# The last mixer of a two-block network: the blocks of one weight matrix in another order, with the attention levels and the convolution's taps placed between them

## The chip, the cores and the metric

The kernel runs on one core of one Trainium2 chip. The core has five engines that run side by side, each through a list of instructions of its own: TensorE (PE in the profile), VectorE (DVE), ScalarE (ACT), GpSimd (POOL) and SyncE (SP, which here only issues DMAs). They meet at semaphores. The metric is the device time of one execution in microseconds. The kernel before took 2451.9 us, the median of three runs between 2444.78 and 2456.0.

## The reference

Two blocks run after each other over 256 tokens of width 1024. The first (two layers of feed-forward, state-space scan and dilated attention) and the experts at the end of the second are not touched here. The change lies in the mixer of the second block:

```python
def hybrid_mixer(u, w_in, w_dw, ...):      # u: 256 tokens x 1024, normalised
    # one product u @ w_in gives: the convolution's input (1024 columns), q and k (512 each),
    # v (1024), r (1024), a low-rank gate (16), the gates of both branches (2048)

def conv_module(u, w_dw, b_dw, ln_g, ln_b, w_pw, b_pw):
    a, gt = jnp.split(u, 2, axis=-1)
    z = a * jax.nn.sigmoid(gt)
    # 31 taps along the tokens, each of the 512 channels by itself, + b_dw
    z = jax.nn.silu(layernorm(z, ln_g, ln_b))
    return z @ w_pw + b_pw

def gla_chunked(q, k, v, logg):            # linear attention, 4 heads, dk 128, dv 256
    b = jnp.cumsum(gc, axis=2)
    diff = b[:, :, :, None, :] - b[:, :, None, :, :]
    decay = jnp.exp(jnp.where(causal, diff, -jnp.inf))
    attn = jnp.einsum("bhid,bhijd,bhjd->bhij", qc, decay, kc)
    o = jnp.einsum("bhij,bhje->bhie", attn, vc)   # and the state that is carried on
```

The output of the attention is divided by its root mean square in each head, multiplied by a gain and by silu(r), and sent through w_gla_o. Both branches are multiplied by their sigmoid gates, added, and sent through w_out.

## The kernel before

Everything in this stage is float32; most activations lie with channels on the 128 partitions and the 256 tokens along each partition. Weights come as blocks of 1024x256 (1 MB) through a ring of four slots (`ring`); SP issues the load of block n+4 once PE has released the slot of block n. PE writes its products to four PSUM banks (`misc`) in a fixed order of "fills", which the list `fills` at the start of `two_blocks` sets: fill m goes to bank m modulo 4, and PE claims it (`claim_bank`) only when fill m-4 has been read out, by ACT or by DVE. No scheduler takes part: each engine's order is the order in which its code is written.

The mixer's parts, by the names in the code:

- **a1, a2** are the low-rank decay. From it DVE and ACT make the log of the decay (`decays2`; ACT's Exp and Ln, then a running sum of 8 scans at L2207, `bcum`).
- **w_in2** is the product with w_in, 24 blocks of 16 matmuls (the profile counts each float32 matmul as two): four of q and k (`qk2`), four of v (`v2`), four of the convolution's input and its gate (`pc`), four of r, eight of gates. ACT reads each out (`evac`).
- **The levels.** The decay between two tokens of a chunk is not one product of a factor per row and one per column that stays in range, so it is built in seven levels (`LEVELS`, halves of 64, 32, ... 1 tokens), one level for the diagonal, and one for what crosses the two halves of 128 tokens (`cross`). For a level DVE takes differences of `bcum` (L2221, L2222), ACT makes their exponential (L1613, `decay_exp`), DVE multiplies them into keys and queries (L2238, L2239), PE forms the products of all pairs (L1040, `pairs`: two fills of four heads), and DVE copies those that the level's mask lets through into `attn` (L2266). `lev_e` and `lev_qk` have two buffers, so level s+2 waits for the products of level s.
- **The taps** (`gated`, L2249 and L2254): 31 taps for each of four groups of channels, 124 instructions on DVE, each waiting for the last one of its own group.
- **o, osum**: the attention's output (L1057 to L1060, read out by ACT at L1651), its squares (DVE, L2278) and their sums by a matmul with ones (L1068). DVE then makes the reciprocal (L2288) and applies it and the gain (L2293, L2296).
- **mean, var**: two matmuls with ones (L1077) for the layer norm of the convolution, with DVE (L2305 to L2317) and ACT (L1658, L1661) around them. Then come the convolution's second product (`pw`, L1089), that of the attention (`ygla`, L799), the merge on DVE, and w_out (L1115).

In the code before, PE goes through all 24 blocks of w_in2, and then through `gla` and the start of `conv_branch`. DVE makes two levels, waits for the pc blocks, does all its 124 taps, and then does the levels that are left one after the other, each with PE and ACT in turn.

Of the kernel before, what the change touches and what calls it, by code (L numbers as in the profile page):

```python
# [8 lines left out]
U32 = mybir.dt.uint32  # L9
ALU = mybir.AluOpType  # L10
# [3 lines left out]
P = 128  # L14
# [35 lines left out]
GH = 4  # L50
# [78 lines left out]
def two_blocks(nc, d, out):  # L129
    fills = []  # L130
    slots, rows_d = [], []
    for l in range(DEPTH):
# [6 lines left out]
        for j in range(8):  # L139
# [8 lines left out]
    fills += [(("mod", 4 * DEPTH - 1), 1), (("norm", U1), 4), ("a1", 1), ("a2", 2), ("qk2", 4), ("v2", 4), ("pc", 4), ("r", 4), ("gates", 8),  # L148
              ("pairs", 2 * len(LEVELS) + 2), ("cross", 1), ("o", GH), ("osum", 2),
              ("mean", 1), ("var", 1), (("pwa", 0), 1), (("pwb", 0), 1), (("pwa", 1), 1), (("pwb", 1), 1), ("ygla", 4), ("garow", 2), (("norm", U1 + 1), 4), ("router", 1),  # L150
# [8 lines left out]
    with ctx:  # L159
# [412 lines left out]
        def _(sp):  # L572
# [111 lines left out]
        def _(pe):  # L684
# [315 lines left out]
            def w_in2():  # L1000
# [5 lines left out]
                for j in range(4):  # L1006
                    cols_out(FILL["qk2"] + j, n0 + j, 0, 0)
# [9 lines left out]
                for j in range(4):  # L1017
                    toks_out(FILL["v2"] + j, n0 + 4 + j, 0, 0)
                for j in range(4):
                    cols_out(FILL["pc"] + j, n0 + 8 + j, 0, 0)  # L1020
                for j in range(4):
                    cols_out(FILL["r"] + j, n0 + 12 + j, 0, 0)
                with pe.Fori(0, 2) as i:
                    for j in range(4):
                        cols_out(FILL["gates"], n0 + 16, i, j)

            def gla():
                for s in range(len(LEVELS) + 1):
                    if s < len(LEVELS):
                        pe.wait_ge(lev_qk_ready, s + 1)  # L1030
                    for t in range(NT):
                        b = claim_bank(FILL["pairs"] + 2 * s + t)
                        for h in range(GH):
                            if s < len(LEVELS):
                                keys = lev_qk[:, s % 2, h * SEQ + t * P:h * SEQ + (t + 1) * P]
                                queries = keys
                            else:
                                keys = q2k2[:, GH + h, t * P:(t + 1) * P]
                                queries = q2k2[:, h, t * P:(t + 1) * P]
                            mm = pe.matmul(b[:, h * P:(h + 1) * P], keys, queries, start=True, stop=True)  # L1040
                        mm.then_inc(filled, 1)
# [7 lines left out]
                for i in range(2 * len(LEVELS) + 2):  # L1049
                    if i >= 2 * len(LEVELS) - 2:  # L1050
                        wait_drained(pe, FILL["pairs"] + i)
                wait_drained(pe, FILL["cross"])
                for h in range(GH):
# [8 lines left out]
                    mm.then_inc(filled, 1)  # L1062
                pe.wait_ge(o_sq, 1)
# [7 lines left out]

            def conv_branch():
                for k, (name, src) in enumerate((("mean", zc), ("var", zsq))):
                    pe.wait_ge(z_out, k + 1)
                    b = claim_bank(FILL[name])
                    for c in range(NC2):
                        mm = pe.matmul(b[:, 0:SEQ], ones[:, :], src[:, c, :], start=(c == 0), stop=(c == NC2 - 1))  # L1077
                    mm.then_inc(filled, 1)
# [236 lines left out]
            gla()  # L1315
# [78 lines left out]
        def _(act):  # L1394
# [220 lines left out]
            def w_in2():  # L1615
                m, n0 = FILL["a1"], RING["win2"]
                wait_filled(act, m)
                act.activation(a1T[0:RANK, :], bank_of(m)[0:RANK, 0:SEQ], ACT.Copy).then_inc(drained[m % 4], 1)
                for j in range(4):
                    evac(FILL["qk2"] + j, n0 + j, q2k2[:, 2 * j:2 * j + 2, :], 2,  # L1620
                         scale=DK ** -0.5 if j < 2 else 1.0)
                for j in range(4):
                    evac(FILL["v2"] + j, n0 + 4 + j, v2[:, :, j * BLK:(j + 1) * BLK], 2)
                    if j == 0:

                        act.wait_ge(gl_ready, 1)
                        s = step(act.activation(lev_e[:, 0, :], lev_e[:, 0, :], ACT.Exp))
                        act.wait_ge(act_step, s)
                        act.activation(lev_e[:, 0, :], lev_e[:, 0, :], ACT.Ln, bias=1.0).then_inc(gl_log, 1)
                for s in range(2):  # L1630
                    decay_exp(s)
                for j in range(4):
                    evac(FILL["pc"] + j, n0 + 8 + j, pc[:, 2 * j:2 * j + 2, :], 2,
                         ACT.Copy if j < 2 else ACT.Sigmoid)
                for j in range(4):
                    evac(FILL["r"] + j, n0 + 12 + j, rT[:, 2 * j:2 * j + 2, :], 2, ACT.Silu)
                with act.Fori(0, 2) as i:
                    for j in range(4):
                        m = FILL["gates"] + j
                        wait_slot_read(act, n0 + 16, i, j)  # L1640
                        act.activation(gT[:, bass.ds(i * 8 + 2 * j, 2), :],
                                       bank_of(m).rearrange("p (a b) -> p a b", a=2), ACT.Sigmoid)\
                            .then_inc(drained[m % 4], 1)

            def gla():
                for s in range(2, len(LEVELS) + 1):
                    decay_exp(s)
# [8 lines left out]
            def conv_branch():  # L1656
                act.wait_ge(var2, 2)
                act.activation(mean, mean, ACT.Sqrt).then_inc(std2, 1)  # L1658
                act.wait_ge(zn_ready, 1)
                for c in range(NC2):  # L1660
                    ins = act.activation(zc[:, c, :], zc[:, c, :], ACT.Silu, scale=colb[:, B_LG + c:B_LG + c + 1],  # L1661
                                         bias=colb[:, B_LB + c:B_LB + c + 1])
                ins.then_inc(zs_ready, 1)
# [120 lines left out]
            gla()  # L1784
            conv_branch()
# [21 lines left out]
        def _(dve):  # L1807
# [375 lines left out]
            def decays2():  # L2183
# [26 lines left out]
                for j in range(4):  # L2210
                    wait_drained(dve, FILL["qk2"] + j)

            def level(s):
# [3 lines left out]
                if s < len(LEVELS):  # L2217
# [3 lines left out]
                    dve.tensor_tensor(ev[:, :, 0:w], mid, bv[:, :, 0:w], ALU.subtract)  # L2221
# [486 lines left out]
```

## Time and profile before

| | |
|---|---|
| median of three runs | 2451.9 us (2444.78 to 2456.0) |
| the profiled execution, whole | 2441.12 us |
| its span, first to last instruction | 2439.3 us |
| PE busy over the span | 2252.6 us, 92% |
| VectorE busy | 1617.8 us, 66% |
| ScalarE busy | 1033.5 us, 42% |
| TensorE's granted clock, mean | 0.961 of full speed |

The profiled execution took 1.8 us more than its span and lies 3.7 us under the fastest of the three runs. In the views below, times are microseconds from the start of the span. A busy share says how long an engine had work in flight, and not that this work set the end. What sets it is read from idle time in front of an instruction, and from what released it (in square brackets in a timeline).

### The profile page before, as it was taken

What the parts mean: (1) busy time and instruction counts of PE and PEld (TensorE: products, weight loads), DVE (VectorE), ACT (ScalarE), POOL (GpSimd) and SP (SyncE); (2) the same over time, 40 slices, a digit from 0 to 9 for tenths busy, and PEclk for the clock granted to TensorE, in tenths of its full rate; (3) what the DMA queues carried; (4) which work ended last, traced back from release to release, by engine and by line L of the source; (5) the groups of instructions that cost most, each with busy time, mean ns of one, the idle gap of its engine ahead of it and who ended that gap; (6) DMA issues with size and microseconds to landing.
All of it is one profiled execution on the core that took longest, in us unless ns stands there. A gap on an engine that the chain in (4) does not pass through costs nothing.

```text
span 2439.3 us, 36349 instructions
## 1 busy us (share of the span) xinstructions
PE 2252.6 (92%) x14222; PEld 1966.0 (81%) x14222; DVE 1617.8 (66%) x2299; ACT 1033.5 (42%) x1209; POOL 440.2 (18%) x227
## 2 busy tenths in 40 slices
PE   5999899999999999999999899859589999999996
PEld 5998897579989988985799788746278888888885
DVE  5655877376576648783766417351488888888887
ACT  3332343244343423432433221110167777777773
POOL 8403471052044034620430000000000000000000
PEclk8999999999999999999999999969699999999998
DMA  8765563166657555541665354304169999999993
GB/s 245 234 194 159 166 196 121 52 228 220 203 179 236 179 166 175 185 144 52 207 215 178 115 155 149 110 0 138 69 200 318 323 315 333 313 331 318 321 326 120
DMA packets 354783, 481.06 MB, mean 197 GB/s; under 512 B 12528, under 2 KB 311808, under 8 KB 354704
## 3 DMA queue, kind: packets, MB, share of 16 engines
q1 hardware_dynamic: 341568, 443.58, 55.8%
q0 software_dynamic: 10496, 34.25, 4.3%
q10 hardware_dynamic: 2640, 2.14, 0.3%
q8 instruction: 54, 0.88, 0.2%
q14 instruction: 25, 0.20, 0.0%
HBM read 478.88 MB, written 1.05 MB: 197 GB/s over the span
## 4 chain that ended last, share of the span: by engine, by line
PE 80%; DVE 14%; ACT 4%; issue 1%; DMA 1%; DVEq 0%; ACTq 0%
PE misc L687 11%; PE misc L689 11%; PE misc L688 11%; PE misc L799 8%; PE acc L957 4%; PE misc L1167 4%; PE misc L1168 4%; PE acc L687 3%; PE acc L689 3%; PE acc L688 3%; PE misc L1153 3%; PE acc L1205 3%; DVE arena L1990 2%; PE misc L1180 2%; DVE ring_low L1874 2%; DVE ring_low L2476 1%
## 5 line engine op out<-in xcount | busy, mean ns | idle before, releaser
L687 PE MATMUL misc<-xl,high_b 128*128 128x256 f32 x1408 | 395.1, 281 | 15.7 <-DVE ring_low L1874 15.7
L688 PE MATMUL misc<-xh,ring_low 128*128 128x256 f32 x1408 | 393.6, 280 | 0.0
L689 PE MATMUL misc<-xh,high_b 128*128 128x256 f32 x1408 | 393.5, 279 | 0.0
L2476 DVE TENSOR_TENSOR ring_low<-ring,high_b 128x2048 fp32r<-128x2048 f32 x128 | 287.4, 2288 | 53.8 <-ACT high_b L1670 53.8
L687 PEld LDWEIGHTS misc<-xl,high_b 128*128 128x128 f32 x1408 | 266.7, 189 | 20.0 <-issue 14.0
L688 PEld LDWEIGHTS misc<-xh,ring_low 128*128 128x128 f32 x1408 | 267.2, 190 | 3.3
L689 PEld LDWEIGHTS misc<-xh,high_b 128*128 128x128 f32 x1408 | 267.9, 190 | 0.0
L1167 PE MATMUL misc<-high_b,ue 128*128 128x256 f32 x1024 | 250.7, 286 | 18.3 <-DVE ring_low L2476 18.3
L799 PE MATMUL misc<-xnT,ring 128*128 128x256 f32 x1152 | 251.9, 381 | 0.0
L1168 PE MATMUL misc<-ring_low,ue 128*128 128x256 f32 x1024 | 247.6, 283 | 0.0
L799 PEld LDWEIGHTS misc<-xnT,ring 128*128 128x128 f32 x1152 | 220.0, 191 | 30.3 <-issue 0.8
L1670 ACT ACTIVATE high_b<-ring 128x2048 fp32r<-128x2048 f32 x128 | 237.8, 1910 | 0.4
L1874 DVE TENSOR_TENSOR ring_low<-ring,high_b 128x2048 fp32r<-128x2048 f32 x88 | 221.4, 2557 | 24.0 <-ACT high_b L1438 24.0
L1469 ACT ACTIVATE arena<-arena 128x256 f32<-128x256 f32 x88 | 36.8, 418 | 435.3 <-DVE arena L1908 435.3
L1167 PEld LDWEIGHTS misc<-high_b,ue 128*128 128x128 f32 x1024 | 195.6, 191 | 24.9 <-issue 21.2
L1168 PEld LDWEIGHTS misc<-ring_low,ue 128*128 128x128 f32 x1024 | 196.2, 192 | 1.6 <-issue 0.2
L1384 POOL TENSOR_SCALAR arena<-arena,cact 128x1024 f32<-128x1024 f32 x56 | 193.5, 3456 | 4.7 <-DMA arena<-in_w_ada_f_dram 1.2
L1381 POOL TENSOR_SCALAR arena<-arena,cact 128x1024 f32<-128x1024 f32 x8 | 26.1, 3261 | 774.6 <-PE misc L997 768.1
L1438 ACT ACTIVATE high_b<-ring 128x2048 fp32r<-128x2048 f32 x88 | 163.1, 1902 | 0.0
L1908 DVE TENSOR_TENSOR arena<-misc,row_rstd 128x256 f32<-128x256 f32 x88 | 37.2, 422 | 188.0 <-PE misc L689 182.2
L1386 POOL TENSOR_TENSOR arena<-arena 128x1024 f32<-128x1024 f32 x56 | 160.1, 2858 | 4.7
L687 PE MATMUL misc<-ring_low,xh 128*128 128x256 f32 x512 | 148.1, 289 | 0.0
(362 smaller groups left out, 4660.9 us busy)
## 6 DMA issues: line engine op xcount, KB each, us to landing
ring<-in_w_dram SPq DMA_DIRECT2D x128, 1024.0 KB, 8.6
ring<-in_w_in_dram SPq DMA_DIRECT2D x72, 1024.0 KB, 5.6
ring_d<-in_w_dram SPq DMA_DIRECT2D x128, 512.0 KB, 4.9
ring<-in_ffn_w_gate_dram SPq DMA_DIRECT2D x44, 1024.0 KB, 5.5
ring<-in_ffn_w_up_dram SPq DMA_DIRECT2D x44, 1024.0 KB, 7.9
ring_d<-in_ffn_w_down_dram SPq DMA_DIRECT2D x88, 512.0 KB, 7.5
arena<-in_w_ada_dram POOLq DMA_DIRECT2D x48, 512.0 KB, 4.9
ring<-in_w_out_dram SPq DMA_DIRECT2D x20, 1024.0 KB, 4.9
```

The costliest lines, as they stand in the source:

```text
L687: pe.matmul(dst, wh, ml, start=start, stop=False, **kw)
L688: pe.matmul(dst, wl, mh, start=False, stop=False, **kw)
L689: return pe.matmul(dst, wh, mh, start=False, stop=stop, **kw)
L799: mm = pe.matmul(b[:, c * SEQ:(c + 1) * SEQ], w[:, k, c * P:(c + 1) * P], src[:, k, :], start=(k == 0), stop=(k == KD - 1))
L1167: pe.matmul(dst, ue[:, k, half, :], high_part(n)[:, k, :], start=(k == 0), stop=False)
L1168: mm = pe.matmul(dst, ue[:, k, half, :], low_part(n)[:, k, :], start=False, stop=(k == KD - 1))
L1384: pool.tensor_scalar(row, row, cact[:, k:k + 1], None, ALU.mult).then_inc(pool_step, 1)
L1386: pool.tensor_tensor(ada, ada, row, ALU.add).then_inc(ada_used, 1)
L1438: act.activation(high_b[:, s, :], ring[:, s, :], ACT.Copy).then_inc(high_in[s], 1)
L1670: act.activation(high_b[:, s, :], ring[:, s, :], ACT.Copy).then_inc(high_in[s], 1)
L1874: dve.tensor_tensor(ring_low[:, s, :], ring[:, s, :], high_b[:, s, :].bitcast(F32), ALU.subtract)\
L2476: dve.tensor_tensor(ring_low[:, s, :], ring[:, s, :], high_b[:, s, :].bitcast(F32), ALU.subtract)\
```

## The change

The same instructions are issued in another order, on PE, ACT and DVE alike; in SP's list of loads the four blocks pc and the four blocks v2 trade places. On PE the blocks pc come before the blocks v2. After each of these eight blocks stands one level's pair of fills, `cross` stands between the blocks r0 and r1, the attention's output after r1, the sums of squares after r3, and the two matmuls of the layer norm behind the third and the fifth block of the gates. DVE makes a level in two parts (`level(s, 0)`, the differences, and `level(s, 1)`, the products) with the copies of the level before the last between them, and takes the taps in portions: 10 at each of levels 4 to 7, then 12, 32 and the last 40. ACT's exponentials stand between its read-outs. The loops over the eight blocks of gates are written out. The diff, cut to its core:

```diff
-    fills += [(("mod", 4 * DEPTH - 1), 1), (("norm", U1), 4), ("a1", 1), ("a2", 2), ("qk2", 4), ("v2", 4), ("pc", 4), ("r", 4), ("gates", 8),
-              ("pairs", 2 * len(LEVELS) + 2), ("cross", 1), ("o", GH), ("osum", 2),
+    fills += [(("mod", 4 * DEPTH - 1), 1), (("norm", U1), 4), ("a1", 1), (("qk2", 0), 1), ("a2", 2)]
+    fills += [(("qk2", j), 1) for j in range(1, 4)]
+    for k in range(len(LEVELS) + 1):
+        fills += [(("pc" if k < 4 else "v2", k % 4), 1), (("pairs", k), 2)]
+    fills += [(("r", 0), 1), ("cross", 1), (("r", 1), 1), ("o", GH), (("r", 2), 1), (("r", 3), 1), ("osum", 2)]
+    fills += [(("gates", j), 1) for j in range(3)] + [("mean", 1), (("gates", 3), 1), (("gates", 4), 1), ("var", 1)]
+    fills += [(("gates", j), 1) for j in range(5, 8)]
...
-                load_block(n0 + 4 + j, 0, 0, w_in, V0 + j * BLK)
+                load_block(n0 + 4 + j, 0, 0, w_in, j * BLK)
             for j in range(4):
-                load_block(n0 + 8 + j, 0, 0, w_in, j * BLK)
+                load_block(n0 + 8 + j, 0, 0, w_in, V0 + j * BLK)
...
+                for k in range(len(LEVELS) + 1):
+                    if k < 4:
+                        cols_out(FILL["pc", k], n0 + 4 + k, 0, 0)
+                    else:
+                        toks_out(FILL["v2", k - 4], n0 + 4 + k, 0, 0)
+                    pairs(k)
+                cols_out(FILL["r", 0], n0 + 12, 0, 0)
+                cross()
+                cols_out(FILL["r", 1], n0 + 13, 0, 0)
+                attended()
+                cols_out(FILL["r", 2], n0 + 14, 0, 0)
+                cols_out(FILL["r", 3], n0 + 15, 0, 0)
+                squares()
+                for j in range(8):
+                    cols_out(FILL["gates", j], n0 + 16 + j, 0, 0)
+                    if j == 2:
+                        moment(0, "mean", zc)
+                    if j == 4:
+                        moment(1, "var", zsq)
...
+            def attended():
+                for k in range(len(LEVELS) + 1):
+                    for t in range(NT):
+                        wait_drained(pe, FILL["pairs", k] + t)
+                for j in range(4):
+                    wait_drained(pe, FILL["v2", j])
...
+                qk2_out(0)
+                qk2_out(1)
+                act.wait_ge(gl_ready, 1)
+                s = step(act.activation(lev_e[:, 0, :], lev_e[:, 0, :], ACT.Exp))
+                act.wait_ge(act_step, s)
+                act.activation(lev_e[:, 0, :], lev_e[:, 0, :], ACT.Ln, bias=1.0).then_inc(gl_log, 1)
+                qk2_out(2)
+                decay_exp(0)
+                decay_exp(1)
+                qk2_out(3)
                 for j in range(4):
+                    evac(FILL["pc", j], n0 + 4 + j, pc[:, 2 * j:2 * j + 2, :], 2, ACT.Copy if j < 2 else ACT.Sigmoid)
+                    decay_exp(j + 2)
                 for j in range(4):
+                    v2_out(j)
+                    if j < 2:
+                        decay_exp(j + 6)
+                r_out(0)
+                r_out(1)
                 for h in range(GH):
                     m = FILL["o"] + h
                     wait_filled(act, m)
                     act.activation(oT[:, 2 * h:2 * h + 2, :], bank_of(m).rearrange("p (a b) -> p a b", a=2),
                                    ACT.Copy).then_inc(drained[m % 4], 1)
+                r_out(2)
+                r_out(3)
                 act.wait_ge(var2, 1)
                 act.activation(rgs, rg, ACT.Sqrt).then_inc(std2, 1)
...
+            def level(s, part_):
...
+            def branches():
+                level(0, 0)
+                level(1, 0)
                 for j in range(4):
+                    wait_drained(dve, FILL["qk2", j])
+                level(0, 1)
+                level(1, 1)
                 last = [0] * NC2
+                taps = iter([(k, c) for k in range(CONV_W) for c in range(NC2)])
+
+                def convolve(n):
...
+                for k in range(len(LEVELS) + 1):
+                    if k + 2 <= len(LEVELS):
+                        dve.wait_ge(lev_qk_ready, k + 1)
+                        level(k + 2, 0)
+                    if k == 4:
+                        for j in range(4):
+                            wait_drained(dve, FILL["pc", j])
+                        link(dve.tensor_tensor(zpad[:, :, CONV_W - 1:], pc[:, 0:NC2, :], pc[:, NC2:2 * NC2, :],
+                                               ALU.mult))
+                    if k >= 4:
+                        convolve(10)
                     for t in range(NT):
+                        m = FILL["pairs", k] + t
                         wait_filled(dve, m)
                         dve.copy_predicated(attn[:, t * GH:(t + 1) * GH, :],
+                                            masks[:, k:k + 1, :].bitcast(U32).to_broadcast([P, GH, P]),
                                             bank_of(m).rearrange("p (a b) -> p a b", a=GH))\
                             .then_inc(drained[m % 4], 1)
                         wait_drained(dve, m)
+                    if k + 2 <= len(LEVELS):
+                        level(k + 2, 1)
+                convolve(12)
                 m = FILL["cross"]
                 wait_filled(dve, m)
                 dve.tensor_copy(across.rearrange("p a b -> p (a b)"), bank_of(m)).then_inc(drained[m % 4], 1)
+                convolve(32)
                 for h in range(GH):
                     wait_drained(dve, FILL["o"] + h)
                 dve.tensor_tensor(osq, oT, oT, ALU.mult).then_inc(o_sq, 1)
+                convolve(CONV_W * NC2)
+                after_step(last[NC2 - 1])
+                dve.nop().then_inc(z_out, 1)
```

On PE, from the first product of w_in2 to the second product of the convolution, the list before reads as follows. L1004 and L1014 are a1 and a2, L799 and L810 blocks of w_in2 (16 matmuls each), L1040 the levels' pairs, L1046 `cross`.

```order
L1004 MATMUL misc<-xnT,wa 16x256 x8
L799 MATMUL misc<-xnT,ring 128x256 x16
L1014 MATMUL misc<-arena,wa 128x256 x4
L799 MATMUL misc<-xnT,ring 128x256 x48
L810 MATMUL misc<-ring,xnT 128x256 x64
L799 MATMUL misc<-xnT,ring 128x256 x128
L1023 UNCONDITIONAL_BRANCH
L1023 ISA
L695 REGISTER_ALU
L799 MATMUL misc<-xnT,ring 128x256 x48
...
L1040 MATMUL misc<-arena 128x128 x64
L1046 MATMUL misc<-arena 128x128 x4
```

In the changed kernel (six lines further down in the file: L805 and L816 are the blocks, L1058 the pairs, L1066 `cross`, L1094 the sums of squares, L1102 mean and var) the same place reads, from the four blocks of q and k on:

```order
L805 MATMUL misc<-xnT,ring 128x256 x64
L1058 MATMUL misc<-arena 128x128 x8
L805 MATMUL misc<-xnT,ring 128x256 x16
L1058 MATMUL misc<-arena 128x128 x8
...
L805 MATMUL misc<-xnT,ring 128x256 x32
L1094 MATMUL misc<-arena,ones 128x256 x8
L805 MATMUL misc<-xnT,ring 128x256 x48
L1102 MATMUL misc<-arena,ones 128x256 x4
L805 MATMUL misc<-xnT,ring 128x256 x32
L1102 MATMUL misc<-arena,ones 128x256 x4
L805 MATMUL misc<-xnT,ring 128x256 x48
L1116 MATMUL misc<-arena,ring 128x256 x32
```

The 64 pairs that stood in one piece behind all blocks now stand in eights between them, and three blocks of gates stand between the last small product and pw (L1116).

On DVE, the place where the taps stood, before (L2246 is the gated input, L2249 and L2254 the taps, L2266 the masked copies):

```order
L2239 TENSOR_TENSOR arena<-arena 128x16x32
L2246 TENSOR_TENSOR arena<-arena 128x4x256 [waits drained3,drained0,drained2,drained1]
L2249 TENSOR_SCALAR arena<-arena,colc,colb 128x256 [waits dve_step]
L2249 TENSOR_SCALAR arena<-arena,colc,colb 128x256 x3
L2254 SCALAR_TENSOR_TENSOR arena<-arena,colc 128x256 [waits dve_step] x120
L2266 COPY_PREDICATED arena<-arena,misc 128x512 [waits dve_step,filled,masks_in]
L2266 COPY_PREDICATED arena<-arena,misc 128x512 [waits filled,drained1]
L2221 TENSOR_TENSOR arena<-arena 128x32x16 [waits drained2]
```

And changed, around level 4 (L2305 is the gated input, L2288 and L2292 the taps, L2312 the masked copies, L2270 and L2271 a level's second part, L2258 and L2260 the first part of `cross`):

```order
L2305 TENSOR_TENSOR arena<-arena 128x4x256 [waits drained3,drained2,drained0,drained1]
L2288 TENSOR_SCALAR arena<-arena,colc,colb 128x256 [waits dve_step]
L2288 TENSOR_SCALAR arena<-arena,colc,colb 128x256 x3
L2292 SCALAR_TENSOR_TENSOR arena<-arena,colc 128x256 [waits dve_step] x6
L2312 COPY_PREDICATED arena<-arena,misc 128x512 [waits filled]
L2312 COPY_PREDICATED arena<-arena,misc 128x512 [waits filled,drained2]
L2270 TENSOR_TENSOR arena<-arena 128x512 [waits filled,lev_exp,drained3]
L2271 TENSOR_TENSOR arena<-arena 128x512
L2258 TENSOR_TENSOR arena<-arena 128x4x128 [waits lev_qk_ready]
L2260 COPY arena<-arena 128x4x128
L2292 SCALAR_TENSOR_TENSOR arena<-arena,colc 128x256 [waits dve_step] x10
```

The first ten taps now stand between two levels, ahead of the copies of level 4; four levels have been through before the first of them.

## Rows read from the trace of the kernel before

**Rows 1.** The page: busy time (share) of each engine, and the granted clock in 40 slices.

```profile
PE 2252.6 (92%) x14222; PEld 1966.0 (81%) x14222; DVE 1617.8 (66%) x2299; ACT 1033.5 (42%) x1209; POOL 440.2 (18%) x227
...
PEclk8999999999999999999999999969699999999998
```

**Rows 2.** Stretches of the span: length, each engine's busy time (instructions), granted clock, DMA.

```profile
core 0: us, PE busy (x) PEld busy (x) DVE busy (x) ACT busy (x) POOL busy (x), PEclk, DMA share, GB/s
1400.00:1562.00 162.00, 162.00 (x750) 142.32 (x749) 61.94 (x147) 26.94 (x34) 0.00 (x0) 1.00 0.48 149
1562.00:1639.00 77.00, 39.32 (x218) 35.03 (x217) 49.14 (x61) 16.49 (x20) 0.00 (x0) 0.73 0.04 14
...
1580.00:1597.00 17.00, 11.81 (x67) 11.13 (x65) 13.36 (x21) 3.17 (x3) 0.00 (x0) 0.70 0.00 0
...
1639.00:1656.00 17.00, 16.73 (x64) 14.29 (x65) 2.63 (x6) 0.22 (x1) 0.00 (x0) 0.82 0.20 62
1656.00:1684.00 28.00, 27.84 (x129) 24.20 (x128) 5.15 (x9) 0.00 (x0) 0.00 (x0) 1.00 0.46 150
```

**Rows 3.** Timeline of PE: start, length, line, tiles, count, idle before and releaser.

```profile
1401.37 1.99 PE L1014 MATMUL misc<-arena,wa 16*128 16x256 f32 x8
1403.29 20.99 PE L799 MATMUL misc<-xnT,ring 128*128 128x256 f32 x96
1424.11 27.79 PE L810 MATMUL misc<-ring,xnT 128*128 128x256 f32 x128
...
1562.24 3.73 PE L1040 MATMUL misc<-arena 128*128 128x128 f32 x32
1568.83 2.74 PE L1040 MATMUL misc<-arena 128*128 128x128 f32 x16 [2.85 <-DVE arena L2239]
...
1606.87 5.41 PE L1068 MATMUL misc<-arena,ones 128*128 128x256 f32 x16 [3.11 <-DVE arena L2278]
...
1629.32 3.78 PE L1077 MATMUL misc<-arena,ones 128*128 128x256 f32 x8 [15.31 <-DVE arena L2308]
1639.28 16.94 PE L1089 MATMUL misc<-arena,ring 128*128 128x256 f32 x64 [6.17 <-ACT arena L1661]
1656.05 27.79 PE L799 MATMUL misc<-arena,ring 128*128 128x256 f32 x128
```

**Rows 4.** Timeline of DVE, same columns.

```profile
1437.84 2.64 DVE L2207 TENSOR_TENSOR_SCAN arena<-arena 128x128 f32<-128x128 f32 x8
...
1483.23 47.59 DVE L2254 SCALAR_TENSOR_TENSOR arena<-arena,colc 128x256 f32<-128x256 f32 x120
1563.40 0.74 DVE L2266 COPY_PREDICATED arena<-arena,misc 128x512 f32<-128x512 uint32 x1 [32.59 <-PE misc L1040]
...
1567.49 0.69 DVE L2238 TENSOR_TENSOR arena<-arena 128x512 f32<-128x512 f32 x1 [1.12 <-ACT arena L1613]
1568.10 0.68 DVE L2239 TENSOR_TENSOR arena<-arena 128x512 f32<-128x512 f32 x1
...
1614.17 6.55 DVE L2288 RECIPROCAL arena<-arena 128x1024 f32<-128x1024 f32 x1 [1.17 <-ACT arena L1654]
1620.76 2.36 DVE L2293 TENSOR_TENSOR arena<-arena 128x1024 f32<-128x1024 f32 x2
1623.16 3.26 DVE L2296 SCALAR_TENSOR_TENSOR arena<-arena,colb 128x256 f32<-128x256 f32 x8
```

**Rows 5.** Timeline of ACT, same columns.

```profile
1417.40 0.60 ACT L1608 ACTIVATE arena<-misc 128x512 f32<-128x512 f32 x1 [6.31 <-PE misc L799]
...
1431.83 1.28 ACT L1627 ACT_TABLE_LOAD   x1
1433.13 1.06 ACT L1627 ACTIVATE arena<-arena 128x1024 f32<-128x1024 f32 x1
...
1637.15 2.07 ACT L1661 ACTIVATE arena<-arena,colb 128x256 f32<-128x256 f32 x4 [1.78 <-DVE arena L2317]
```

**Rows 6.** DMA issues between 1380 and 1700: count, KB each, median time to landing.

```profile
ring<-in_w_in_dram SPq DMA_DIRECT2D x20, 1024.0 KB, 5.4
```

More of the change, by code:

```diff
@@ new lines, in w_in2, with pairs @@
+                squares()
[5 more added lines that the diff above has]
+                        moment(1, "var", zsq)
+            def pairs(k):
+                if k == len(LEVELS):
+                    for j in range(4):
+                        wait_drained(pe, FILL["qk2", j])
+                else:
+                    pe.wait_ge(lev_qk_ready, k + 1)
+                for t in range(NT):
+                    b = claim_bank(FILL["pairs", k] + t)
+                    for h in range(GH):
+                        if k < len(LEVELS):
+                            keys = lev_qk[:, k % 2, h * SEQ + t * P:h * SEQ + (t + 1) * P]
+                            queries = keys
+                        else:
+                            keys = q2k2[:, GH + h, t * P:(t + 1) * P]
+                            queries = q2k2[:, h, t * P:(t + 1) * P]
+                        mm = pe.matmul(b[:, h * P:(h + 1) * P], keys, queries, start=True, stop=True)
+                    mm.then_inc(filled, 1)
@@ L1042, in gla, with cross @@
+            def cross():
                 pe.wait_ge(lev_qk_ready, len(LEVELS) + 1)
@@ L1070, in gla, with moment @@
                     mm.then_inc(filled, 1)
-            def conv_branch():
[L1073 to L1078, printed above, removed]
+            def moment(k, name, src):
+                pe.wait_ge(z_out, k + 1)
+                b = claim_bank(FILL[name])
+                for c in range(NC2):
+                    mm = pe.matmul(b[:, 0:SEQ], ones[:, :], src[:, c, :], start=(c == 0), stop=(c == NC2 - 1))
+                mm.then_inc(filled, 1)
+            def conv_branch():
                 pe.wait_ge(zs_ready, 1)
@@ L1618, in w_in2, with qk2_out, v2_out, r_out @@
                 act.activation(a1T[0:RANK, :], bank_of(m)[0:RANK, 0:SEQ], ACT.Copy).then_inc(drained[m % 4], 1)
+                def qk2_out(j):
+                    evac(FILL["qk2", j], n0 + j, q2k2[:, 2 * j:2 * j + 2, :], 2, scale=DK ** -0.5 if j < 2 else 1.0)
+                def v2_out(j):
+                    evac(FILL["v2", j], n0 + 8 + j, v2[:, :, j * BLK:(j + 1) * BLK], 2)
+                def r_out(j):
+                    evac(FILL["r", j], n0 + 12 + j, rT[:, 2 * j:2 * j + 2, :], 2, ACT.Silu)
@@ L1632, in w_in2 @@
[L1632 to L1643, printed above, removed]
@@ L1652, in gla @@
                                    ACT.Copy).then_inc(drained[m % 4], 1)
+                r_out(2)
+                r_out(3)
                 act.wait_ge(var2, 1)
                 act.activation(rgs, rg, ACT.Sqrt).then_inc(std2, 1)
[L1656 to L1663, printed above, removed]
+                for j in range(8):
+                    evac(FILL["gates", j], n0 + 16 + j, gT[:, 2 * j:2 * j + 2, :], 2, ACT.Sigmoid)
+                    if j == 4:
+                        act.wait_ge(var2, 2)
+                        act.activation(mean, mean, ACT.Sqrt).then_inc(std2, 1)
+                    if j == 6:
+                        act.wait_ge(zn_ready, 1)
+                        for c in range(NC2):
+                            ins = act.activation(zc[:, c, :], zc[:, c, :], ACT.Silu,
+                                                 scale=colb[:, B_LG + c:B_LG + c + 1],
+                                                 bias=colb[:, B_LB + c:B_LB + c + 1])
+                        ins.then_inc(zs_ready, 1)
             def gathered_experts():
@@ L2260, in gla @@
-            def gla():
-                dve.wait_ge(masks_in, 16)
-                for s in range(len(LEVELS) + 1):
+                taps = iter([(k, c) for k in range(CONV_W) for c in range(NC2)])
+                def convolve(n):
+                    for k, c in itertools.islice(taps, n):
+                        if k == 0:
+                            last[c] = step(dve.tensor_scalar(zc[:, c, :], zpad[:, c, 0:SEQ], colc[:, c:c + 1],
+                                                             colb[:, B_DW + c:B_DW + c + 1], ALU.mult, ALU.add))
+                        else:
+                            after_step(last[c])
+                            last[c] = step(dve.scalar_tensor_tensor(
+                                out=zc[:, c, :], in0=zpad[:, c, k:k + SEQ],
+                                scalar=colc[:, k * NC2 + c:k * NC2 + c + 1], in1=zc[:, c, :],
+                                op0=ALU.mult, op1=ALU.add))
@@ L2657, in _ @@
             decays2()
-            level(0)
-            level(1)
-            gated()
-            gla()
-            conv_branch()
+            branches()
             merge()
```

98 lines of the change are left out of this document (21 added, 77 removed).

## The prediction

> **What bounds the kernel now.** I read four views, each narrower than the last. First the page: TensorE (PE) is busy 92% of the span, and of the 40 slices of 61 us only the first, the last and two behind the middle (0.6 each, the 27th and the 29th) have a granted clock under 0.9 [rows 1]. The reader is to see where PE is not at speed: the 27th slice begins at 1586 us and lies in the stage of this change, the 29th behind w_out. Second the stretches: from 1400 to 1562 us PE works without a gap at clock 1.00, while VectorE (DVE) is busy 61.94 of 162 us and ScalarE (ACT) 26.94; from 1562 to 1639 PE is busy 39.32 of 77 us, at a mean clock of 0.73, and DVE 49.14 [rows 2]. So first PE alone sets the pace beside a DVE that idles, and then a chain of DVE, ACT and PE does, in turns. Third PE's own timeline: twenty blocks of w_in2 run from 1424.11 to 1562.24, 138.13 us or 6.907 each (32 counted matmuls, 0.216 each); then come the levels with an idle of 2.85 us before one of them, and later idles of 3.11, 15.31 and 6.17, each released by DVE or ACT, before pw starts at 1639.28 [rows 3]. Fourth DVE's and ACT's timelines. The 120 multiply-add taps take 47.59 us in one piece, 0.397 each; then DVE waits 32.59 us for the first pairs, which it could have had long before, since PE came to them only behind all 24 blocks [rows 4]. The two long engines' works are laid end to end, not beside each other.
>
> **What PE has to do, in either order.** The change removes and adds no matmul. Behind the twenty blocks stand, by counted instructions: eight levels of 16 and cross with 8 (136), the output with 48, the sums of squares with 16, mean and var with 8 each. At full clock the 128-column kind takes 3.73/32 = 0.117 us [rows 3], so 184 x 0.117 = 21.5; the 256-column kind 0.216, so 32 x 0.216 = 6.9. Together 28.4 us. Today PE needs 1639.28 - 1562.24 = 77.0 for them. If PE never waits in the new order, pw starts at 1562.24 + 28.4 = 1590.6, which is 48.7 earlier. Then pw itself: 64 matmuls take 16.77 us today (1639.28 to 1656.05), because they start at a lowered clock (0.82, [rows 2]); at 0.216 they take 13.8. That is another 3.0. Sum 51.6 us.
>
> **Does PE wait in the new order?** I follow the new lists with durations from the rows. The times are on the axis of before, which holds up to 1410.
>
> The start. ACT reads out the second block of q and k at 1410.5 (one block ahead of the read-out at 1417.40, [rows 5]) until 1411.1. Exp and Ln stand right behind it now, not behind the first v block. From the Exp's start to the scans' start it is 1437.84 - 1433.13 = 4.7 us [rows 4, 5]; with the table load of 1.28 ahead, the scans start at 1417.1 and end 2.64 later, at 1419.8. Four differences at the spacing of 0.61 (1567.49 to 1568.10) end at 1422.2, the two exponentials at about 1423.4, the fourth read-out at 1424.9, and the products of level 0 at 1426.2. PE comes to the first pairs at 1424.1 + 6.9 = 1431.0: 4.8 us to spare.
>
> The levels. PE takes 6.91 + 16 x 0.117 = 8.8 us for a block and a level. DVE has in it two differences (1.2), two copies (1.5, [rows 4]), two products (1.2): 3.9 us; from level 4 on also 10 taps (4.0), and once the gated input (about 1.2): 9.1 at the worst, 7.9 at the next. Level k+2 is ready some 3 to 4 us after the pairs of level k, and PE wants it two blocks and one level later, 15.7 us: about 12 to spare. PSUM is the other hold: a block claims the bank of the fill four before, which is the second copy of the level before the last, done 7 us earlier. What I price at nothing here (10 + 10 + 10 + 10 taps, 16 us, inside a queue for which PE waits) is hidden by the 8.8 us that PE itself takes per level; without that cover the taps would fall on PE one for one.
>
> The tail. PE: eight levels end at 1494.3, r0 1501.2, cross 1502.2, r1 1509.1, output 1514.7, r2 and r3 1528.5, squares' sums 1532.0, three gates 1552.7, mean 1554.4, two gates 1568.2, var 1569.9, three gates 1590.6. DVE: 12 taps and the copy of cross to 1502.9, 32 taps to 1515.6, squares to 1517.9 (wanted at 1528.5), 40 taps to 1533.8 (mean wants them at 1552.7), then the reciprocal 6.55, products 2.36 and gain 3.26 [rows 4] to about 1548.7, wanted by ygla after 1604. Mean's work on DVE, some 3 us, ends near 1557.3 and var wants it at 1568.2. Behind var stands today an idle of 6.17, of which 2.07 are the Silu [rows 3, 5]: so the normalised input is there at about 1574. The Silu, though, stands behind the read-out of the seventh gate block (1584.5): with table load 1.28 and 2.07 it ends at 1587.9, and pw wants it at 1590.6. **2.7 us to spare, the thinnest place of all.** The queue behind that waiting ACT instruction holds only the last gates' read-out, for which DVE's merge waits after pw's first fills.
>
> **Weights.** pc and v2 are loaded in the new order by SP, equal in size. 1 MB lands in 5.4 us [rows 6]; a slot released is needed again three blocks, 20.7 us, later. Eight blocks now have 8.8 us each instead of 6.9, which asks less of the queue; pw, ygla and w_out follow without the pause they had, at one MB in 6.9 us as w_in2 always had at DMA share 0.48 [rows 2]. No term.
>
> **What the trace doesn't show** is PE going back and forth between blocks and small matmuls. The nearest row is a2: 8 instructions of the 256-column kind between two blocks take 1403.29 - 1401.37 = 1.92, where 8 x 0.216 = 1.73 [rows 3]. So 0.19 us per inserted piece, 13 pieces, 2.5 us at one end; at the other the 0.117 contains the last matmul's drain, and overlapped pieces would give back up to 1.5. I take nothing, since between pieces without a wait the rows show none.
>
> The Trainium skill (ScalarE: Activation LUTs, What ACT_TABLE_LOAD costs) says a switch of function set costs a load of about 1.28 us and a drain of about 1.38 on top. Here the Exp starts 1.30 us after its load starts [rows 5]: load yes, drain no. By the page the Silu would end 1.4 us later, still ahead of PE, so the sum is the same and the thin place thinner.
>
> **Sum.** 2441.12 - 51.6 = 2389.5 us for an execution like the profiled one. That one lay 10.8 under the median of the runs; on the median's scale it is 2451.9 - 51.6 = 2400.3. I say 2400.
>
> **Rivals.**
> - *The convolution's tail is late* (0.08). The Silu's place has 2.7 us; a DVE that falls more than 10 us behind, or an ACT that falls 3 behind, makes PE wait there. For it: the DVE queue is one file, and a tap waits for its own predecessor. Against: every link up to the Silu has over 10 us. Price: the last idle of 6.17 comes back and with it pw's lowered clock (3.0): 2409.4. All of the last two idles (15.31 as well) would give 2424.8; 0.02 for that.
> - *Slower: PE's clock falls in the mixed stretch* (0.03). Where PE stops briefly for each level, its mean clock is 0.70, between its two levels of 1.2 and 2.4 GHz (1580 to 1597, [rows 2]). If PE stopped at the levels for a moment each time, the big blocks would run at the low clock too. The work from 1424.11 to the end of pw is 138.1 + 28.4 + 13.8 = 180.3 us at full clock and takes 231.9 today; it breaks even at a mean clock of 0.78. At 0.70 it takes 257.6: 25.7 later, 2477.6. Against: it needs stops, and I find none above; while fed, the clock stays at 1.00 for 162 us. The Trainium skill (TensorE: Matmul & The Clock Gate, A second HAM failure mode) tells of just this, brief idles between groups that cycle through PSUM banks making the clock swing. The small idles with a clock of 0.70 agree; the blocks, which also cycle through the four banks, do not.
> - *No change* (0.02): weights come late as PE no longer pauses, and the gain goes into waits for slots. It would take 51.6/30 = 1.7 us at each of the 30 blocks from pc to w_out, so landings of over 22 us instead of 5.4. 2452.
>
> **Numbers.** The forecast has 0.85. About 0.5%, 12 us, is what a measurement of this kernel tells from no change. The forecast's own spread: the runs lie from 7 under to 4 over their median, the switches cost up to 2.5. Low end 2389, where runs come out like the profiled one; high end 2414, which takes in the late tail with the runs' 4 us. Faster 0.95 (forecast and tail), same 0.02, slower 0.03.
>
> **What would show it.** Right: PE at clock 1.00 without an idle over 1 us from 1401 to the end of ygla, the twenty blocks and the small pieces in about 167 us, pw in 13.8, DVE's taps in five or more portions with the first before the copies of level 4, and the stages behind w_out as long as before. Wrong: an idle of PE before a level's pairs (start too late), before pw (the Silu), a granted clock under 1.00 beside blocks, or a longer expert stage.

## The result: 2386.4 us against 2448.3, just under the range

The changed kernel took 2386.41 us (median of four runs, 2381.95 to 2391.17); the kernel before, now with four runs, 2448.34 (2439.75 to 2456.0). The ratio is 0.9748, with an interval of 0.9708 to 0.9789. That is faster, as forecast, but 13.6 us under the predicted 2400 and 2.6 us under the low end of the range. The profiled execution of the changed kernel took 2391.17 us, where the sum for an execution like the profiled one had been 2389.5. That they lie so close is in part luck: this execution came to the stretch that the change touches 4.3 us later than the profiled one of before (1405.67 against 1401.37).

The page of the changed kernel, busy time and granted clock. They answer to [rows 1]:

```profile
PE 2244.2 (94%) x14222; PEld 1962.4 (82%) x14222; DVE 1615.0 (68%) x2299; ACT 1038.7 (43%) x1213; POOL 443.5 (19%) x227
...
PEclk8999999999989999999999989999699999999998
```

The instruction counts of PE and DVE are the same as before; ACT has four table loads more. One of the two slices at clock 0.6, the 27th, is gone; the two new eights (12th and 24th slice) come from ahead of the changed stretch, which begins at 1405.67, inside the 24th, and has clock 1.00 throughout. The stretch from a2 to the start of the attention's second product (L805 on oT, "ygla"), in both kernels; columns as in [rows 2]. Before:

```profile
1401.37:1656.05 254.68, 216.73 (x1025) 190.73 (x1025) 113.71 (x214) 43.66 (x54) 0.00 (x0) 0.91 0.33 103
```

After:

```profile
1405.67:1607.81 202.14, 202.14 (x1025) 180.14 (x1025) 113.60 (x214) 48.34 (x58) 0.00 (x0) 1.00 0.42 130
```

The same 1025 matmul records, and the same 113.6 us of DVE; but PE is busy for all of the 202.14 us, at clock 1.00. The stretch is 52.54 us shorter: 37.95 us are idle that PE no longer has (254.68 - 216.73), and 14.59 are busy time (216.73 - 202.14), the same matmuls at clock 1.00 instead of a mean of 0.91. Where [rows 3] showed idles of 2.85, 3.11, 15.31 and 6.17, PE's timeline after the change shows none (excerpts; L805 and L816 are the blocks, L1058 the levels, L1102 mean and var, L1116 pw):

```profile
1407.59 27.89 PE L805 MATMUL misc<-xnT,ring 128*128 128x256 f32 x128
1435.32 1.95 PE L1058 MATMUL misc<-arena 128*128 128x128 f32 x16
1437.11 7.07 PE L805 MATMUL misc<-xnT,ring 128*128 128x256 f32 x32
1444.01 1.95 PE L1058 MATMUL misc<-arena 128*128 128x128 f32 x16
...
1571.55 1.89 PE L1102 MATMUL misc<-arena,ones 128*128 128x256 f32 x8
1573.28 20.88 PE L805 MATMUL misc<-xnT,ring 128*128 128x256 f32 x96
1594.00 13.98 PE L1116 MATMUL misc<-arena,ring 128*128 128x256 f32 x64
1607.81 27.79 PE L805 MATMUL misc<-arena,ring 128*128 128x256 f32 x128
```

No row has a bracket, which would show an idle of PE. A level costs PE 1.79 us (1435.32 to 1437.11), and pw 13.81 where it took 16.77. DVE around level 4, where the taps begin (L2305 gated input, L2288 and L2292 taps, L2312 masked copies), answers to [rows 4]:

```profile
1467.07 1.22 DVE L2305 TENSOR_TENSOR arena<-arena 128x1024 f32<-128x1024 f32 x1
1468.33 1.38 DVE L2288 TENSOR_SCALAR arena<-arena,colc,colb 128x256 f32<-128x256 f32 x4
1469.62 2.46 DVE L2292 SCALAR_TENSOR_TENSOR arena<-arena,colc 128x256 f32<-128x256 f32 x6
1472.00 1.48 DVE L2312 COPY_PREDICATED arena<-arena,misc 128x512 f32<-128x512 uint32 x2
...
1482.82 4.04 DVE L2292 SCALAR_TENSOR_TENSOR arena<-arena,colc 128x256 f32<-128x256 f32 x10
1488.57 0.73 DVE L2312 COPY_PREDICATED arena<-arena,misc 128x512 f32<-128x512 uint32 x1 [1.71 <-PE misc L1058]
```

The idle in the brackets has changed sides: DVE now waits for PE, by 1.71 us in the last row. Only at level 4 itself is DVE the later one: PE began its next block at 1471.88, and the copies, which stand behind the first ten taps, began at 1472.00. Last the thinnest place, ACT's Silu (L1691), which answers to [rows 5]:

```profile
1587.29 0.60 ACT L1634 ACTIVATE arena<-misc 128x512 f32<-128x512 f32 x1 [6.31 <-PE misc L805]
1587.91 1.28 ACT L1691 ACT_TABLE_LOAD   x1
1589.20 2.07 ACT L1691 ACTIVATE arena<-arena,colb 128x256 f32<-128x256 f32 x4
```

It ends at 1591.27, and pw starts at 1594.00: 2.7 us to spare. The table load costs its 1.28 us and no drain on top: the Silu starts 1.29 us after the load does.

### The profile page after: what moved, and what is told of

The parts are those of the page before. It is cut to its first block, busy times and chain, and to the rows that moved or that the text cites. A ratio compares the mean times of both kernels' runs of the same rounds, so it can differ in the third digit from the quotient of the medians.

```text
span 2389.3 us, 36341 instructions
## 1 busy us (share of the span) xinstructions
PE 2244.2 (94%) x14222; PEld 1962.4 (82%) x14222; DVE 1615.0 (68%) x2299; ACT 1038.7 (43%) x1213; POOL 443.5 (19%) x227
## 4 chain that ended last, share of the span: by engine, by line
PE 83%; DVE 12%; ACT 3%; issue 1%; DMA 1%; DVEq 0%; ACTq 0%
PE misc L693 11%; PE misc L695 11%; PE misc L694 11%; PE misc L805 8%; PE misc L1194 4%; PE acc L963 4%; PE misc L1195 4%; PE acc L693 3%; PE acc L694 3%; PE acc L695 3%; PE misc L1180 3%; PE acc L1232 3%; DVE arena L2019 2%; PE misc L1207 2%; DVE ring_low L1903 2%; DVE ring_low L2525 1%
## 5 line engine op out<-in xcount | busy, mean ns | idle before, releaser
L805 PE MATMUL misc<-xnT,ring 128*128 128x256 f32 x1152 | 251.5, 379 | 0.0
L805 PEld LDWEIGHTS misc<-xnT,ring 128*128 128x128 f32 x1152 | 217.9, 190 | 29.9 <-issue 0.8
```

The costliest lines, as they stand in the source:

```text
L805: mm = pe.matmul(b[:, c * SEQ:(c + 1) * SEQ], w[:, k, c * P:(c + 1) * P], src[:, k, :], start=(k == 0), stop=(k == KD - 1))
```

## The experiments

The mechanism was as forecast, the time was not. Theory S: the mixer stretch is 52.5 us shorter, and the 62 us between the first medians hold a chance high in the few runs of before. Rival G: in most executions the change gains 8 to 10 us more in some other place. In what follows the indented texts are what was expected before a run, and brackets behind a median hold its lowest and highest run or, from the third version on, its ratio to the kernel before with the 95% interval.

**The changed kernel again, and the kernel before again**, both unaltered, five rounds. Nothing is edited.

> The changed kernel, unaltered. Theory S: the mixer stretch, from the products of a2 to the start of the attention's second product, is 52.5 us shorter (254.7 to 202.1 in the two traces) and nothing else is; what the first comparison showed beyond it (62 us between the medians) is scatter of stages that the change doesn't touch. Then five rounds give a difference of medians of 50 to 57 us, a ratio near 0.978, and the stretch in this trace is again 202.1 within 0.5. Rival G: the change gains some 8 to 10 us more outside the stretch in most executions. Then the difference is again 60 us or more, the ratio near 0.975.

> The kernel before, unaltered, timed against itself. Theory S: ratio 1.000 with an interval of some 0.3% either way, single executions spread over 10 us or more, the mixer stretch 254.7 us again within 0.5, and the difference to the first trace lies before 1380 us, in the first block. Rival G says nothing of this run except that its scatter should be small beside 8 us: all executions within 5 us.

Measured: the changed kernel 2386.84 us (2381.77 to 2388.89), the kernel before 2441.66 (17 runs, 2437.61 to 2450.72) beside it and 2442.65 (12 runs, 2434.2 to 2452.2) as a kernel of its own. Ratio of the changed kernel 0.9774 (0.9759 to 0.9788), a difference of 54.8 us; ratio of before to itself 1.0002 (0.9986 to 1.0017). The changed kernel's median moved by 0.4 us against the first comparison, that of before fell by 6.7. So S holds in the main, and G falls: the first runs of the kernel before were high. That they were so by chance alone is not shown. Of the 29 runs above one reached 2451.9, the median of the first three, so those three were an unlikely draw; the changed kernel's first four were not high. Why the three were is open. The two new traces, first row and last row of the stretch, of the changed kernel:

```profile
1396.37 1.99 PE L1020 MATMUL misc<-arena,wa 16*128 16x256 f32 x8
...
1598.51 27.79 PE L805 MATMUL misc<-arena,ring 128*128 128x256 f32 x128
```

and of the kernel before:

```profile
1407.21 1.99 PE L1014 MATMUL misc<-arena,wa 16*128 16x256 f32 x8
...
1662.58 27.79 PE L799 MATMUL misc<-arena,ring 128*128 128x256 f32 x128
```

The stretch is 202.14 us again, to the hundredth, and 255.37. The latter is 0.69 more than the 254.68 of the first trace, where 0.5 had been allowed: in these traces the stretch with idles in it repeated less closely than the one without. The spans are 2380.0 and 2446.0, 66 us apart: 53.2 in the stretch, 10.8 in what comes before it, which both kernels have alike, and 1.9 behind it. Over the ten traces of this study the stretch begins between 1396.29 and 1407.94, in no order that follows the kernel. The last transpose of `xt` in the first block (L846, in the changed kernel L852) starts between 969.0 and 979.3 in them, in nearly the same order, so most of that scatter is there already; its cause is not known.

A difference behind the stretch is in both pairs of traces, 1.8 and 1.9 us. It lies in the router's 32 small matmuls. Before:

```profile
1730.00:1737.00 7.00, 6.80 (x32) 6.83 (x32) 0.00 (x0) 0.42 (x1) 0.00 (x0) 0.50 0.00 0
```

After:

```profile
1681.90:1687.20 5.30, 5.25 (x32) 5.12 (x32) 0.00 (x0) 0.28 (x1) 0.00 (x0) 0.68 0.00 0
```

The granted clock is 0.50 (1.2 GHz) all through them before. After, it is 1.00 (2.4 GHz) as they begin and 0.50 again two microseconds later, a mean of 0.68:

```profile
1682.00:1683.00 1.00, 1.00 (x10) 1.00 (x11) 0.00 (x0) 0.18 (x1) 0.00 (x0) 1.00 0.00 0
1684.00:1685.00 1.00, 1.00 (x6) 1.00 (x7) 0.00 (x0) 0.00 (x0) 0.00 (x0) 0.50 0.00 0
```

The idles ahead of them are equal in both (10.38 and 1.29 us). Neither theory had this; S had said that nothing outside the stretch is shorter.

**Which parts of the new order are needed: the taps behind the levels.**

```diff
-                    if k >= 4:
-                        convolve(10)
...
+                for j in range(4):
+                    wait_drained(dve, FILL["pc", j])
+                link(dve.tensor_tensor(zpad[:, :, CONV_W - 1:], pc[:, 0:NC2, :], pc[:, NC2:2 * NC2, :], ALU.mult))
                 convolve(12)
```

> The changed kernel, but the gated input and the first 40 taps stand behind the last level instead of at levels 4 to 7; 80 taps then stand between the squares and the read-out of the sums of squares. Theory (PE waits only where a queue in front of it is longer than its own work): DVE reads the sums out at about 1553.3 on the axis of the changed kernel's trace, but PE wants that PSUM bank for the third block of gates at 1549.1: an idle of 4.9 us there, nothing elsewhere, so 4 to 6 us slower than the changed kernel. Rival (taps may stand anywhere before mean wants them): 0. Rival (taps have to be cut into the levels to be hidden at all): 16 us or more.

Measured: 2391.33 us (0.9786, 0.9772 to 0.9799), 4.5 over the changed kernel; the stretch took 208.94 us, 6.8 more, which is over the 4 to 6 worked out. PE at the third block of gates:

```profile
1535.56 13.98 PE L805 MATMUL misc<-xnT,ring 128*128 128x256 f32 x64
1554.45 8.78 PE L805 MATMUL misc<-xnT,ring 128*128 128x256 f32 x32 [4.92 <-DVE arena L2329]
```

The idle of 4.92 is there, where it was worked out, and L2329 is the read-out of the sums of squares: the wait is for a PSUM bank, not for data. What the expectation left out is the block behind it: 8.6 us instead of 6.9, at a mean clock of 0.81. Both rivals fall: 6.8 us is neither 0 nor 16.

**The order of the blocks undone**, v2 before pc, with all taps behind the levels and the bank of the sums of squares emptied in time.

```diff
-                    if k < 4:
-                        cols_out(FILL["pc", k], n0 + 4 + k, 0, 0)
-                    else:
-                        toks_out(FILL["v2", k - 4], n0 + 4 + k, 0, 0)
+                    if k < 4:
+                        toks_out(FILL["v2", k], n0 + 4 + k, 0, 0)
+                    else:
+                        cols_out(FILL["pc", k - 4], n0 + 4 + k, 0, 0)
...
                 dve.tensor_tensor(osq, oT, oT, ALU.mult).then_inc(o_sq, 1)
-                convolve(CONV_W * NC2)
+                convolve(32)
```

> The order of the blocks undone (v2 before pc again), the gated input and all taps behind the last level, in portions of 12, 32, 32 and 48, with the read-out of the sums of squares ahead of the last 48. Theory: the block order is not needed; every wait keeps 0.7 us or more, so within 1 us of the changed kernel in the mixer stretch (202 us). Rival (the block order carries a part of the gain, since it lets the taps start earlier): 5 us or more slower than the changed kernel.

Measured: 2383.1 us (0.9759, 0.9745 to 0.9772), and the stretch 202.14 us, the same as the changed kernel's:

```profile
1402.12:1604.26 202.14, 202.14 (x1026) 180.13 (x1025) 113.66 (x214) 44.29 (x55) 0.00 (x0) 1.00 0.42 130
```

The block order and the four tens of taps at levels 4 to 7 carry nothing. The 3.7 us between the medians are not in the stretch, and the intervals of the two ratios overlap.

**All taps in one piece at level 4.**

```diff
-                    if k >= 4:
-                        convolve(10)
+                    if k == 4:
+                        convolve(CONV_W * NC2)
```

> The changed kernel with all 124 taps at level 4 instead of in portions from there on. Theory (what stands in DVE's queue ahead of a level falls on PE once it is longer than what PE has left to do): DVE is in the taps from 1468.3 to 1517.5 on the axis of the changed kernel's trace. PE can do the first fill of level 5 and then needs the bank that DVE empties behind the taps: idle from 1479.7 to 1518.3, 38.6 us, and some 3 us of a block at the low clock behind it: 41 to 43 us slower than the changed kernel, which leaves a gain of about 13 us. Rival (two level buffers and four banks cover it): under 10 us slower.

The last four versions, from this one on, were timed in another session, in which the kernel before had a median of 2442.3; the changed kernel was not timed again there.

Measured: 2425.97 us (0.9939, 0.9919 to 0.9959); the stretch 243.25 us, 41.1 more. PE:

```profile
1472.62 1.05 PE L1058 MATMUL misc<-arena 128*128 128x128 f32 x8
1511.73 2.07 PE L1058 MATMUL misc<-arena 128*128 128x128 f32 x8 [38.05 <-DVE arena L2312]
1513.60 8.99 PE L816 MATMUL misc<-ring,xnT 128*128 128x256 f32 x32
```

One fill of level 5 goes, the other waits 38.05 us for the bank behind DVE's 49 us of taps. The same instructions, moved ahead in one engine's list, take back 41.1 of the 52.5 us. The rival falls.

**Mean and var ahead of the gates.**

```diff
+                moment(0, "mean", zc)
+                moment(1, "var", zsq)
                 for j in range(8):
                     cols_out(FILL["gates", j], n0 + 16 + j, 0, 0)
-                    if j == 2:
-                        moment(0, "mean", zc)
-                    if j == 4:
-                        moment(1, "var", zsq)
```

> The changed kernel with the two matmuls of the layer norm right behind the sums of squares, ahead of all gates. Theory: mean waits 2.1 us for the last tap, and var waits until DVE has been through the reciprocal, its products and the mean (1537.5 to 1555.2): some 16 us idle. With some 3 us of the next block at the low clock, 20 to 22 us slower than the changed kernel. Rival (ACT and DVE are fast enough beside PE, only the levels mattered): under 5 us.

Measured: 2403.73 us (0.9846, 0.9828 to 0.9863), 16.9 over the changed kernel's median; the stretch in the trace 223.32 us, 21.2 more. PE:

```profile
1539.73 1.99 PE L1099 MATMUL misc<-arena,ones 128*128 128x256 f32 x8 [2.01 <-DVEq L2326]
1557.38 3.78 PE L1099 MATMUL misc<-arena,ones 128*128 128x256 f32 x8 [15.65 <-DVE arena L2354]
```

Idles of 2.01 and 15.65, as worked out, and the stretch is within the 20 to 22; the median is not. The rival falls by either. So the blocks of gates between the small matmuls are their cover.

**The Silu one read-out later.**

```diff
-                    if j == 6:
+                    if j == 7:
                         act.wait_ge(zn_ready, 1)
```

> The changed kernel with the convolution's Silu behind the read-out of the eighth block of gates instead of the seventh. Theory: it ends at 1594.8 + 1.3 + 2.1 = 1598.2 on the axis of the changed kernel's trace and pw, which could start at 1594.0, waits 4.2 us; 4 to 6 us slower than the changed kernel in the mixer stretch. Rival (the margin of 2.7 us at this place was not real): a difference outside 3 to 8 us.

Measured: 2394.49 us (0.9816, 0.9797 to 0.9836); the stretch 208.17 us, 6.0 more.

```profile
1588.86 15.77 PE L1116 MATMUL misc<-arena,ring 128*128 128x256 f32 x64 [4.07 <-ACT arena L1691]
```

The wait is 4.07 us, and pw takes 15.60 instead of 13.81 behind it. The margin was real: a read-out that comes 6.9 us later, less a margin of 2.7, gives 4.2.

**Half of the change: levels and taps between the blocks, the tail behind them as before.**

```diff
-                attended()
                 cols_out(FILL["r", 2], n0 + 14, 0, 0)
                 cols_out(FILL["r", 3], n0 + 15, 0, 0)
-                squares()
                 for j in range(8):
                     cols_out(FILL["gates", j], n0 + 16 + j, 0, 0)
...
+                attended()
+                squares()
+                moment(0, "mean", zc)
+                moment(1, "var", zsq)
```

> Half of the change: the levels and all taps stand between the blocks, but the attention's output, the sums of squares, mean and var stand behind the last block of gates, as before. Theory: from the output's first matmul to pw it takes again what it took before, 41.1 us (1598.16 to 1639.28), of which PE works 12.4 at full speed, and pw starts at the lowered clock again (3.0): some 31 us slower than the changed kernel, so the levels' part of the gain is some 23 us and the tail's 31. Rival (the levels are nearly all of the gain): under 10 us slower than the changed kernel.

Measured: 2420.11 us (0.9913, 0.9894 to 0.9932); the stretch 233.96 us, 31.8 more.

```profile
1591.20 5.41 PE L1091 MATMUL misc<-arena,ones 128*128 128x256 f32 x16 [3.11 <-DVE arena L2321]
...
1613.65 3.78 PE L1099 MATMUL misc<-arena,ones 128*128 128x256 f32 x8 [15.32 <-DVE arena L2349]
```

The idles of [rows 3] are back, 3.11 and 15.32. So of the 52.5 us, the levels between the blocks bring 20.7 and the tail between the gates 31.8. The part with fewer matmuls (80 records against the levels' 136) brings more, because PE stood idle longer in it: 24.6 us (3.11, 15.32 and 6.17) of the 37.95, above all behind DVE's reciprocal and products ahead of the second small matmul.

**Medians beside traces.** Against the changed kernel's 2386.84 the six medians lie 4.5, -3.7, 39.1, 16.9, 7.7 and 33.3 us higher, in the order above; the stretches in the traces are longer by 6.8, 0, 41.1, 21.2, 6.0 and 31.8. The two differ by up to 4.3 us, with four or five executions to a median and one trace to a version. The waits and their places rest on the traces; the medians bear out their size within those 4 us. The Silu's median, 7.7 over, misses the 4 to 6 worked out and stays within the rival's 3 to 8.

No version has a shorter stretch than the changed kernel: PE has no idle left in it to remove.

## Why the prediction was right in its mechanism and wrong in its time

- **What bounds the kernel, and that PE never waits in the new order**: right. The first level was said to have 4.8 us to spare; its products ended at 1430.7 and PE came at 1435.3, 4.6. The Silu 2.7: measured 2.7. The squares were ready 10.3 us before PE wanted them, mean's input 18.7 and var's 10.7, where 10.6, 18.9 and 10.9 had been worked out.
- **The sum, 51.6**: 52.5 in the stretch. The 128-column matmuls were taken at 0.117 us, with the drain of the last in it; between blocks they take 1.79/16 = 0.112. That 0.9 us is the overlap between pieces, for which the prediction had allowed up to 1.5 and taken nothing; the 2.5 at the other end did not come. The router's 1.8 was in no term: the "stages behind w_out as long as before" was wrong by that.
- **The step that failed** is the last one, "on the median's scale it is 2451.9 - 51.6 = 2400.3". It took the median of three runs for the kernel's level, and took the profiled execution for one that "lay 10.8 under the median of the runs". With 17 runs the level of the kernel before is 2441.7, and the profiled execution, at 2441.12, lay on it. What made the three first runs high stays open, as said above. 2441.7 - 51.6 = 2390.1; measured were 2386.4 and 2386.8. Of the 13.6 us missed, 10.2 are this step, 2.7 the two terms above, and the rest is within the scatter.
- **The low end, 2389**, was set where "runs come out like the profiled one", as if nothing could come out lower. Runs of before reach from 2434 to 2452, some 8 below and 10 above their level; a range round 2390 had to begin near 2382.
- **Rivals**: the late tail did not happen; its mechanism is real, as the Silu's and the bank's experiments show, and its price was right in kind: a wait (4.07 us), and 1.8 us of lowered clock behind it where the prediction had 3.0 for a wait of 6.17. The clock stayed at 1.00 through the whole mixed stretch, so the slower rival never began. The Trainium skill (TensorE: Matmul & The Clock Gate, A second HAM failure mode) is not contradicted: it speaks of brief idles between groups, and the new order has none. Where an experiment made an idle of 4.07 us, pw behind it ran at a mean clock of 0.89. Weights were never late: PE had no idle at all in the stretch.

## What to carry to other kernels

When one engine has long work that needs nothing, and others have a chain with it in turns, place the long work's pieces between the chain's steps, and check each queue and each buffer's release for what stands ahead, as the bank of the sums of squares shows, which cost 4.92 us of idle when 80 taps stood ahead of its read-out. The tail of a stage, with the slow steps on the other engines, may bring more than the loop that looks larger. And a forecast rests on the level of the kernel before as much as on its sum: three runs that scatter by 11 us did not give it here, and where the profiled execution lies under all of them, as here, both levels belong in the range, with the scatter on either side.

## What the runs showed of the hardware that was not expected

An idle of PE costs more than itself. One of 4.92 us was followed by a block of 8.62 us instead of 6.91 (granted clock 0.81), one of 4.07 us by 15.60 instead of 13.81 for pw (0.89). The loss did not grow with the idle in proportion. Behind 38.05 us it was 2.9 (1.87 instead of 0.89 for a fill, and 8.82 instead of 6.91 for the block behind it). Behind 15.65 us it was 3.1 (3.57 instead of 1.73 for var, and 56.50 instead of 55.25 for the eight blocks of gates). Behind 2.01 us there was next to none: mean ran at clock 1.00.

The router's small matmuls, behind the same idles of 10.38 and 1.29 us, took 7.01 us in three of the ten traces (the two of before and the one with the tail as before) and 4.6 to 5.5 in the other seven. So a change in one stage went with one or two microseconds in another, through the clock. In the trace with the late Silu, where they took 4.61, small matmuls further on took longer, and all that lies behind the stretch came to 782.5 us, against 781.4 to 781.6 in the other six and 783.1 to 783.4 in the three. Why the clock rose ahead of the router in the seven and not in the three is open.
